# Forgetting attention on one core: units taken two at a time, products with p two units behind

## The reference

```python
s = jnp.einsum('bqhd,bkhd->bhqk', q_blk, k_all, preferred_element_type=jnp.float32)
s = s + fq_blk.transpose(0, 2, 1)[..., None] - f_k[:, :, None, :]
s = jnp.where((kpos[None, :] <= qpos[:, None])[None, None], s, -jnp.inf)
p = jax.nn.softmax(s, axis=-1)
return jnp.einsum('bhqk,bkhd->bqhd', p.astype(v_all.dtype), v_all)
```

## Time and profile before

| | us |
|---|---|
| median of 3 runs | 3189.69 |
| lowest, highest | 3185.55, 3195.04 |
| profiled execution | 3188.47 |
| its span | 3186.8 |
| attention in it | 2041 to 2906 |

### The profile page before, as it was taken

How to read it: one execution, slowest core, us unless ns; L and a number is a source line. 1 busy time by engine, 2 the same in 40 slices (tenths; PEclk the granted TensorE clock), 3 DMA queues, 4 the chain that set the end, 5 groups by cost and what they waited for, 6 DMA issues and landing times. The chain is left out here.

```text
span 3186.8 us, 43017 instructions
## 1 busy us (share of the span) xinstructions
PE 2895.5 (91%) x15730; PEld 2008.2 (63%) x15730; DVE 1533.9 (48%) x3562; ACT 952.5 (30%) x1547; POOL 750.7 (24%) x428
## 2 busy tenths in 40 slices
PE   5589999997899978999979999799999989995999
PEld 2367777776777856777757777344444444442757
DVE  1542222212877638431173125667766766763343
ACT  0322212212555544210042111144334334433000
POOL 1310000000000003000030000476767667676000
PEclk8589999998999988999989999699999999997999
DMA  9532222213565524121153221513421331303764
GB/s 340 187 87 79 54 86 80 77 47 126 178 217 189 158 95 174 73 77 48 40 178 80 73 48 53 157 35 104 114 76 51 104 92 42 107 32 124 247 199 133
DMA packets 281946, 355.41 MB, mean 112 GB/s; under 512 B 40044, under 2 KB 172460, under 8 KB 281681
## 3 DMA queue, kind: packets, MB, share of 16 engines
q1 hardware_dynamic: 279364, 344.23, 34.0%
q0 software_dynamic: 2304, 8.39, 0.7%
q10 hardware_dynamic: 72, 0.07, 0.0%
HBM read 250.28 MB, written 102.10 MB: 111 GB/s over the span
## 5 line engine op out<-in xcount | busy, mean ns | idle before, releaser
L2318 POOL TENSOR_TENSOR at_p_sum<-at_p_sum,at_p 128x1024 f32<-128x1024 f32 (+3 forms) x264 | 541.7, 2052 | 95.9 <-ACT at_p L2174 84.6
L2174 ACT ACTIVATE at_p<-psum 128x1024 f32<-128x1024 f32 (+1 forms) x320 | 286.9, 897 | 516.6 <-PE psum L2014 514.1
L2220 DVE CUSTOM_DVE_ANT_0 psum<-psum,at_f_wide 128x512 f32<-128x512 f32 (+3 forms) x640 | 376.8, 631 | 0.0
L2094 PE MATMUL psum<-at_p,at_v 128*64 128x512 f32 (+3 forms) x1280 | 305.9, 557 | 0.1
L672 POOL TENSOR_TENSOR kv_h_lo<-kv_aux,kv_h_hi 128x512 fp32r<-128x512 f32 x16 | 24.1, 1507 | 1056.8 <-ACT kv_h_hi L649 1025.9
L768 PE MATMUL psum<-kv_w_hi,kv_h_hi 128*128 128x512 f32 x512 | 201.2, 393 | 13.2 <-DVE kv_w_lo L964 13.2
L768 PE MATMUL psum<-gla_w_hi,gla_h_hi 128*128 128x512 f32 x512 | 201.3, 393 | 2.7 <-DVE gla_w_lo L964 2.7
L769 PE MATMUL psum<-kv_w_lo,kv_h_hi 128*128 128x512 f32 x512 | 200.2, 391 | 0.0
L770 PE MATMUL psum<-kv_w_hi,kv_h_lo 128*128 128x512 f32 x512 | 200.0, 391 | 0.0
L769 PE MATMUL psum<-gla_w_lo,gla_h_hi 128*128 128x512 f32 x512 | 199.5, 390 | 0.0
L770 PE MATMUL psum<-gla_w_hi,gla_h_lo 128*128 128x512 f32 x512 | 199.3, 389 | 0.0
(11 more groups left out here) (425 smaller groups left out, 6088.3 us busy)
## 6 DMA issues: line engine op xcount, KB each, us to landing
mod_w<-in_ada_w SPq DMA_DIRECT2D x12, 2048.0 KB, 18.0
at_f_wide<-F SPq DMA_DIRECT2D x32, 512.0 KB, 5.9
at_page<-in_cache_k SPq DMA_DIRECT2D x32, 512.0 KB, 3.4
gla_w_raw<-in_gla_w_in SPq DMA_DIRECT2D x6, 2048.0 KB, 8.0
mod_w<-in_kv_ada_w SPq DMA_DIRECT2D x4, 2048.0 KB, 10.0
v_gla<-gla_stage SPq DMA_DIRECT2D x32, 256.0 KB, 2.0
sg_gla<-gla_stage SPq DMA_DIRECT2D x32, 256.0 KB, 2.0
gl_sg<-sg_gla SPq DMA_DIRECT2D x16, 512.0 KB, 3.9
```

What stands on the lines that cost most here:

```text
L2094: mm = pe.matmul(bank_o[half[a], skip:NB], v[u][:, i, half[a]], p_tile[e % PT][:, a, skip:NB], start=(i == 0), stop=(i == R * G + R - 1), ...
L2174: act.activation(p_tile[e % PT][:, :, skip:NB], pair_of(bank_st[e % 2])[:, :, skip:NB], ACT.Exp)\
L2220: op = dve.tensor_tensor_reduce(pair_of(at(n))[:, a, 0:w], pair_of(at(n))[:, a, 0:w], f_wide[:, a, c * NB:c * NB + w], 1.0, -3.0e38, ALU.s ...
L2318: pool.tensor_tensor(p_sum[s][:, :, skip:NB], p_sum[s][:, :, skip:NB], p_tile[e % PT][:, :, skip:NB], ALU.add).then_inc(p_added, 1)
```

## The change

Units are taken two at a time, e and e + 1 with e even (called a couple here).

- PE waits for the exponential of e - 1 once, sets the masks of both units, makes the maximum of slot e, the logits of e and of e + 1, the maximum of slot e + 1, the job of slot e, `weigh_v` of e - 2 and e - 1, and the job of slot e + 1.
- The last two products with p of a head pair are made in the first couple of the next one, and so is ACT's copy of group 3.
- The slot number UN is gone. Its m row goes to slot 0 of the next head pair (`CARRIED`).
- ACT takes both exponentials, then the jobs of slot e, the copy, and the jobs of slot e + 1.
- DVE takes both maxima, then the jobs of both slots, then the page jobs of both.
- SP asks for `max_full` 3 ahead instead of 1 where it loads the next head pair's forget values and V.

PE (and the table of slots and SP's wait):

```diff
-    turn_slots = {2: (LAST, "sum", 3, 0), 3: (LAST, "pick", 3, 0), 4: (LAST, "spread", 3, 0),
+    turn_slots = {0: (CARRIED, "m_row", 2, 0), 2: (LAST, "sum", 3, 0), 3: (LAST, "pick", 3, 0), 4: (LAST, "spread", 3, 0),
...
-                  32: (NEXT, "turn", 3, 0), 35: (NEXT, "turn", 3, 1), UN: (NEXT, "m_row", 2, 0)}
+                  32: (NEXT, "turn", 3, 0), 35: (NEXT, "turn", 3, 1)}
...
-                        sp.wait_ge(max_full, UN * (2 * j + u) + AHEAD + 1)
+                        sp.wait_ge(max_full, UN * (2 * j + u) + AHEAD + 3)
...
-                    pe.wait_ge(p_ready, UN * h + e + 1)
+                    pe.wait_ge(p_ready, UN * h + e + 2)
...
+                def max_unit(j, u, e):
+
+                    for who, kind, t, c, n in slots_of(j, u)[e]:
+                        if kind == "max":
+                            at = whose(who, j, u)
+                            max_wait(*at, t, c, n)
+                            if c == t // R:
+                                masks(bank_max, t % R * P, g.hide_qk)
+                            maxima(*at, t, c)
+
+                def turn_unit(j, u, e):
+
+                    for who, kind, a, b, n in slots_of(j, u)[e]:
+                        turn_op(*whose(who, j, u), before(j, u), kind, a, b, n)
+
+                def two_units(j, u, e):
+
+                    logits_wait(j, u, e)
+                    for s in (e, e + 1):
+                        G, i = exp_units[s]
                         if i >= R * G:
-                            masks(bank_st[e % 2], (i - R * G) * P, g.hide_kq)
-                    for at, t, c, n in maxes:
-                        if c == t // R:
-                            max_wait(*at, t, c, n)
-                            masks(bank_max, t % R * P, g.hide_qk)
-                    for at, t, c, n in maxes:
-                        if c != t // R:
-                            max_wait(*at, t, c, n)
-                        maxima(*at, t, c)
-                    if e < UN:
-                        logits(j, u, e)
-                    for who, kind, a, b, n in slot:
-                        turn_op(*whose(who, j, u), before(j, u), kind, a, b, n)
+                            masks(bank_st[s % 2], (i - R * G) * P, g.hide_kq)
+                    max_unit(j, u, e)
+                    logits(j, u, e)
+                    logits(j, u, e + 1)
+                    max_unit(j, u, e + 1)
+                    turn_unit(j, u, e)
                     if e:
+                        weigh_v(j, u, e - 2)
                         weigh_v(j, u, e - 1)
+                    elif not is_first(j, u):
+                        weigh_v(*previous(j, u), UN - 2)
+                        weigh_v(*previous(j, u), UN - 1)
+                    turn_unit(j, u, e + 1)
...
+                weigh_v(PAIRS // 2 - 1, 1, UN - 2)
+                weigh_v(PAIRS // 2 - 1, 1, UN - 1)
```

ACT:

```diff
-                    for e in range(UN + 1):
-                        if e < UN:
-                            exponential(j, u, e)
+                    for e in range(0, UN, 2):
+                        exponential(j, u, e)
+                        exponential(j, u, e + 1)
                         for who, kind, a, b, n in slots_of(j, u)[e]:
                             filler(*whose(who, j, u), before(j, u), kind, a, b, n)
-                        for G in range(NG):
+                        if e == 0 and not is_first(j, u):
+                            copy_o(*previous(j, u), NG - 1)
+                        for G in range(NG - 1):
                             if units_to(G) == e:
                                 copy_o(j, u, G)
+                        for who, kind, a, b, n in slots_of(j, u)[e + 1]:
+                            filler(*whose(who, j, u), before(j, u), kind, a, b, n)
```

DVE:

```diff
-                    for e in range(UN + 1):
-                        for who, kind, a, b, n in slots_of(j, u)[e]:
-                            turn_op(*whose(who, j, u), before(j, u), kind, a, b, n)
-                        if e in page_at:
-                            score_page(j, u, page_at.index(e))
+                    for e in range(0, UN, 2):
+                        for kinds in (("max", "m_max"), ("turn", "m_row", "sum", "pick", "spread")):
+                            for s in (e, e + 1):
+                                for who, kind, a, b, n in slots_of(j, u)[s]:
+                                    if kind in kinds:
+                                        turn_op(*whose(who, j, u), before(j, u), kind, a, b, n)
+                        for s in (e, e + 1):
+                            if s in page_at:
+                                score_page(j, u, page_at.index(s))
```

23 lines of the change are left out of this document (9 added, 14 removed).

## The result

The changed kernel takes 3228.12 us (median of four runs, 3222.58 to 3237.66) where the kernel before takes 3188.71 (3185.55 to 3195.04). The profiled execution of the changed kernel is the slowest of its four, with a span of 3236.0 us against 3186.8.

What follows compares the result with a forecast made beforehand. The prediction took PE, with its changes of weight shape, to bound the attention. From 3188.5 us it added 27 for queues (PE's gain against new waits for DVE) and 20 for the falling clock: 3235 us, range 3202 to 3262.

Steps and rivals of the forecast that it cites:

- The gain on PE: PE's order in attention: fewer changes of weight shape save 5.9 us per head pair, masks and old waits counted in.
- x: Time of each middle pass among four p-matmul passes in a row on PE: bounded between 0.43 and 0.48 us.
- The waits: PE waiting for DVE's chunk maxima: 13.6 us per head pair where 3.3 were; net queues +27 us.
- turns of units 9, 13, 25, 35: Odd-unit turns, with transposes behind the p matmuls, delay the next maximum: 5.3 us together per head pair.
- couples 10 and 20: An odd unit's turn plus a page product on DVE: waits of 2.4 to 3.0 us each, taken 5.0.
- couples 0 and 32: A page product alone behind the second maximum: 0.5 to 0.8 us each, more behind couple 0; taken 1.5 for both.
- picks, m rows and all else: Six picks and m rows on odd units or couple 0, some 0.3 us each: 1.8 us per head pair.
- T + 1.9: When DVE is through with a couple's second maximum, T being that maximum's start on PE.
- The clock: PE's clock falls to half speed behind long waits: 12 more falls, 1.7 us lost each, +20 us.
- rival 1: PE's clock holds because waits are in pieces too short; only the +27 us remain: 3216 us, chance 0.25.
- rival 2: DVE keeps up, so waits stay small: -55 us, 3134 us; chance 0.07 for faster, 0.08 for within 0.3%.
- rival 3: Half of DVE's page products last 3.6 instead of 1.8 us against POOL's adds: +25 us more, 3260, chance 0.10.

Runs made afterwards that it cites:

- e5: Changed kernel with cached-page scores left out and each maximum taken over its first 128 columns alone: 3122.42 us, ratio 0.9781 to the kernel before.
- e6: Kernel before with cached-page scores left out and each maximum taken over its first 128 columns alone: 3147.46 us, ratio 0.9861.
- e2: Changed kernel with DVE's page products and reductions replaced by tiny instructions with the same semaphores: 3189.65 us, ratio 0.9981 to the kernel before.
- e4: Changed kernel with DVE's page jobs moved between a couple's two maxima, nothing left out: 3188.99 us, ratio 0.9983 to the kernel before.
- e9: Changed kernel with page jobs between the two maxima and a new table of job places: 3164.96 us, ratio 0.9903 to the kernel before.
- e12: e9 with the copy that spreads 1/sum written as a reduction over a length-one axis: 3134.48 us, ratio 0.9813 to the kernel before.

## Why the prediction was right, and where its steps were off

**The gain on PE: right in kind, a quarter too large.** Fewer changes of shape are what it comes from: counted in the traces, the attention has 1029 before and 690 after. x is 0.43 us, the lower bound; I had taken a value just above. A full couple is thus 4.38 us as worked out. Over eight head pairs I had 5.9 x 8 = 47 us; the traces show 35.8, and 42.1 between e5 and e6, where waits are few.

The 47 itself rests on a miscount. I had 8 masks of maxima with an odd number; the trace has 10 per head pair directly behind logits (2 in the last head pair). Such a mask takes about half of a couple's gain: from the first logits of units 30 and 31 to those of the next couple it is 5.10 us before and 4.73 after, with units 32 and 33, where the mask stands, 5.44 and 5.26. And in units 21, 23 and 39 the kernel before has both masks side by side, so that the change of 0.10 is saved in 5 couples and not in 8. With the measured x that gives -20 x 0.36 + 10 x 0.2 - 5 x 0.1 = -5.7 us per head pair, 46 over eight: next to my 47 only because the errors cancel (and 8 x 0.2 - 8 x 0.10 is 0.8 besides, not the 0.7 of the prediction).

What is missing from it in the traces is mostly this: a wait costs more than its idle time. In the rows below PE idles for 0.17 us ahead of the maximum at 2379.46. In the stream that maximum would have come at 2377.29 + 8 x 0.23 = 2379.13, 0.33 earlier, and the p matmuls follow it after 0.43 instead of 0.33: 0.26 us beyond the idle.

```profile
2378.90 0.39 PE L2014 MATMUL psum<-at_q_more,at_k_more 64*128 64x512 f32 x2
2379.46 0.49 PE L2014 MATMUL psum<-at_kT_hi,at_qT_hi 64*128 64x512 f32 x2 [0.17 <-DVE at_chunk_max L2238]
2379.89 0.65 PE L2094 MATMUL psum<-at_p,at_v 128*64 128x512 f32 x2
```

That is one place. Over whole kernels it is less: PE's own time is 762.1 us in e5 with 29 waits for chunk maxima and 770.7 in the changed kernel with 107, and 804.2 in e6 with 1 and 806.5 before with 28, some 0.1 us per wait. With this estimate the 28 waits that e5 has more than e6 are 3 us and the 79 that the changed kernel has more than the one before are 8, and both gains come to 44 or 45 us. The kernels compared differ in more than their waits, so 0.1 is an estimate and was not measured by itself.

**The waits: the sum right, its parts not.** 13.6 us per head pair were worked out; 12.7 to 14.1 were measured in the first seven and 4.7 in the last, 95.5 in all, inside the 80 to 110 that I had named. The parts, per head pair from the second to the seventh:

| wait behind | worked out us | measured us |
|---|---|---|
| turns of units 9, 13, 25, 35 | 5.3 | 3.3 |
| couples 10 and 20 | 5.0 | 3.6 |
| couples 0 and 32 | 1.5 | 3.0 |
| picks, m rows and all else | 1.8 | 2.8 |

So two parts were about a third too dear and two too cheap, and the sum came out by luck. In the third head pair:

```profile
2283.18 2.65 DVE L2262 TENSOR_TENSOR at_page<-at_page,at_q_sample 128x1024 f32<-128x1024 f32 x1
...
2287.27 0.50 PE L2014 MATMUL psum<-at_kT_hi,at_qT_hi 64*128 64x512 f32 x2 [3.03 <-DVE at_chunk_max L2238]
...
2311.85 0.50 PE L2014 MATMUL psum<-at_kT_hi,at_qT_hi 64*128 64x512 f32 x2 [1.26 <-DVE at_chunk_max L2238]
...
2315.86 1.22 DVE L2262 TENSOR_TENSOR at_page<-at_page,at_q_sample 128x1024 f32<-128x1024 f32 x1
...
2317.71 0.28 PE L2008 MATMUL psum<-hide_qk,ident 128*128 128x128 bf16 x2 [0.86 <-DVE at_chunk_max L2238]
...
2344.18 0.69 DVE L2227 TENSOR_TENSOR at_qT_lo<-psum,at_qT_hi 128x512 fp32r<-128x512 f32 x1 [2.41 <-ACT at_qT_hi L2178]
...
2344.79 1.59 DVE L2262 TENSOR_TENSOR at_page<-at_page,at_q_sample 128x1024 f32<-128x1024 f32 x1
...
2347.82 0.28 PE L2008 MATMUL psum<-hide_qk,ident 128*128 128x128 bf16 x2 [2.77 <-DVE at_chunk_max L2238]
```

The 1.26 us at 2311.85 stand behind the turn of unit 9, priced 0.8 and 0.9 for narrow units. Couple 20 (the last three rows) goes as told: the low part, then the product behind it, then the maximum, and PE waits 2.77 us, in the 2.4 to 3.0. Couple 10 does not: 0.86 us. Its product met no add of POOL and lasted 1.22, and the maximum that stood behind it is one of 128 columns, for which DVE needs 0.7 us (2316.99 to 2317.65, with the reads) and not 1.47; I had priced every maximum as 512 wide. The longest wait is behind couple 0, 3.03 us, where I had 0.75: its product is issued 0.25 us into an add of POOL of 1.82 us and took 2.65, beyond anything in the trace of before, and the diagonal units give PE less work meanwhile. I had named both in a half sentence and then taken 1.5 for couples 0 and 32 together. The mechanism (DVE's jobs behind the second maximum against 0.2 us of room) is shown by e2 and e4: 45 us come back when the page jobs are cut down, and 44 when they only move. What was too narrow in it is that I put the next maximum behind all jobs and never asked what the other gap, ahead of the second maximum, could hold. (Its "T + 1.9" should be T + 2.0 by its own 0.54 and 1.47; no wait in the sum hangs on it by more than 0.1.)

**The clock: right, slightly too dear.** 14 stretches at 0.50 where 4 were. I had 12 falls and +20 us on top of before; it is 10 stretches more and 13.6 us, since two of before's stretches, 10.2 us each, stood at the loop's border. The length of a wait doesn't by itself decide: most falls stand behind gaps of 2.4 to 3.5 us, but gaps of 2.77 (2345.0) and 2.78 us (2812.6) had none, two falls stand behind 1.26 and 1.58 us (2426.3 and 2865.6), and in e9 two stand behind 1.13 us. A forecast of so many falls is good as a mean and not for one place.

**What was not in the sum.** The standstill at the loop's border made two head pairs of before some 6 us longer each, with the clock behind it (113.8 and 114.1 against 107 to 108), about 13 us in all; in the changed kernel PE stands there for 1.7 us each time. It was in the profile, in PE's waits, and I had counted only waits for chunk maxima.

**The sum of it.** The forecast had +47 us: -47 of PE's own time, +74 of new waits with the last head pair's share taken off, +20 of the clock. In the attention it is +38.8: -35.8, +61.0 (68.8 more for chunk maxima, about 7 less at the loop's border, which I had not seen) and +13.6. Term by term that is 11 us too little gain, 13 us too much wait and 6 us too much clock, and they cancel to 8. The direction and the path (DVE's jobs behind the second maximum, then the clock) are borne out by the runs; that 3228 lies only 7 us from 3235 is in part luck.

**The rivals.** The holding clock (rival 1) fell with the 14 stretches at half clock. DVE did not keep up (rival 2), but e4, e9 and e12 show that the case existed once DVE's jobs stand elsewhere: e12 takes 3134 us. That it is the very number of this rival is chance, since e12 also has a new table of places and the reduction. Long products (rival 3) came behind couple 0 only, 2.04 to 2.71 us in the second to seventh head pair, and twice in the last; none lasted 3.6, and over all 32 the mean even fell, from 1795 to 1714 ns. What I had as a stretch of unknown size has an exact form, the rest of the running add plus 1.08 us, and could have been read from the trace of before, where 31 of 31 products keep it. PE's wait behind couple 0, 2.4 to 3.1 us, is nevertheless in part this rival's.

## What to carry to other kernels

When two stages' work is batched to save an engine's changes of shape, write down what the other engine's queue holds between two uses of a shared buffer: the batch moves the moments at which a side job can stand for free, and the side jobs have to move with it (here DVE had two gaps of about 0.7 us per couple and the changed order used one; 44 us lay in where eight page jobs stood in a head pair, and with all work done couples beat the kernel before only after these and the rest had moved). A DVE instruction that reads two SBUF operands or copies SBUF to SBUF should be priced as what is left of the running GpSimd instruction plus its own time; where GpSimd is always busy, a slower form that doesn't share, as a reduction, is the faster one. And split a stage into idle time, time at low clock and the rest before comparing kernels: the rest is what an edit to the bound engine changes, and it is steady enough to predict from.
